# Finishing a mixture-of-experts block: last weights in two transfers, residual carried into the accumulators, final norm read from PSUM

## The reference, cut to what matters

```python
def moe_swiglu(h, router, w1, w3, w2):
    ...
    gate = jnp.sum(jax.nn.one_hot(top_i, N_EXPERTS, dtype=jnp.float32) * top_p[..., None], axis=1).astype(h.dtype)
    y = jnp.zeros_like(t)
    for e in range(N_EXPERTS):
        y = y + gate[:, e:e + 1] * swiglu(t, w1[e], w3[e], w2[e])
    return y.reshape(b, s, d)
...
            x = x + moe_swiglu(h, moe_router[j], moe_w1[j], moe_w3[j], moe_w2[j])
    return rmsnorm(x, final_norm_g)
```

## Time and profile before

| | us |
|---|---|
| median of 3 runs | 1676.49 |
| lowest and highest | 1676.17, 1682.53 |
| profiled execution, first to last instruction (span) | 1673.1 |
| end of the last scaling by VectorE in it | 1670.04 |

### The profile page before, as it was taken

One profiled execution on the slowest core, in us unless ns is written; L12 is line 12 of the kernel. 1 busy time (PEld: TensorE's weight loads), 2 busy tenths in 40 slices (PEclk: granted clock), 3 DMA queues, 4 the chain that ended last, 5 costly groups with the idle time before them and its releaser, 6 DMA issues.

```text
span 1673.1 us, 34751 instructions
## 1 busy us (share of the span) xinstructions
PE 1614.6 (97%) x15676; PEld 1089.6 (65%) x15676; DVE 612.5 (37%) x1036; ACT 446.8 (27%) x693; POOL 32.3 (2%) x27
## 2 busy tenths in 40 slices
PE   6999999999999999999999999999999999899995
PEld 6987776899988987776866534565345643356431
DVE  3678775554644677766501010101101010010101
ACT  3564533453534554523201010000100010000101
POOL 0000030000000000030000000000000000000000
PEclk9999999999999999999999999999999999999998
DMA  6424312454654433413989999999999999999994
GB/s 254 177 101 149 140 60 106 153 201 165 243 197 142 162 124 132 146 52 134 429 307 353 383 429 428 424 427 425 428 427 425 424 427 427 427 426 424 426 429 168
DMA packets 41108, 472.75 MB, mean 283 GB/s; under 512 B 4544, under 2 KB 4544, under 8 KB 5632
## 3 DMA queue, kind: packets, MB, share of 16 engines
q1 hardware_dynamic: 40592, 468.86, 69.6%
q0 software_dynamic: 368, 1.65, 0.2%
HBM read 469.44 MB, written 1.05 MB: 281 GB/s over the span
## 4 chain that ended last, share of the span: by engine, by line
PE 85%; DMA 7%; DVE 4%; ACT 2%; issue 1%; SPq 0%; DVEq 0%; ACTq 0%
PE bank L608 72%; DMA pairs_high<-stream 4%; DMA pairs_low<-stream 2%; PE bank L1221 1%; PE bank L1285 1%; PE bank L690 1%; DVE ring_a_r L1708 1%; DVE arena L1708 1%; PE bank L984 1%; ACT high_a L1378 1%; DMA smalls<-small 1%; PE bank L895 1%; PE bank L976 1%; PE bank L804 0%; PE bank L1246 0%
## 5 line engine op out<-in xcount | busy, mean ns | idle before, releaser
L608 PE MATMUL bank<-pairs_high,hsel 128*32 128x256 f32 (+1 forms) x4320 | 334.6, 408 | 2.8 <-DMA pairs_high<-stream 2.8
L608 PEld LDWEIGHTS bank<-pairs_high,hsel 128*32 128x32 f32 (+1 forms) x4320 | 161.7, 113 | 159.9 <-issue 83.2
L1708 DVE TENSOR_TENSOR ring_a_r<-ring_a,high_a 128x2048 fp32r<-128x2048 f32 x82 | 188.0, 2297 | 125.7 <-ACT high_a L1378 125.6
L1708 DVE TENSOR_TENSOR arena<-arena,bank 128x256 f32<-128x256 f32 (+2 forms) x122 | 44.5, 392 | 464.2 <-ACT arena L1631 451.4
L1378 ACT ACTIVATE high_a<-ring_a 128x2048 fp32r<-128x2048 f32 x82 | 157.1, 1916 | 134.4 <-PE bank L608 117.1
L608 PE MATMUL bank<-pairs_high,actT 128*32 128x256 f32 (+1 forms) x2048 | 165.2, 413 | 7.7 <-DMA pairs_high<-stream 7.7
L608 PE MATMUL bank<-hT_h,ring_a_r 128*128 128x256 f32 (+1 forms) x592 | 167.4, 283 | 0.0
L608 PE MATMUL bank<-high_a,hT_h 128*128 128x512 f32 (+1 forms) x416 | 165.1, 397 | 0.8 <-issue 0.8
L608 PE MATMUL bank<-pairs_low,hsel 128*32 128x256 f32 (+1 forms) x1952 | 161.9, 415 | 0.2 <-DMA pairs_low<-stream 0.2
L608 PE MATMUL bank<-high_a,hT_l 128*128 128x512 f32 (+1 forms) x416 | 160.1, 385 | 0.0
L608 PE MATMUL bank<-ring_a_r,hT_h 128*128 128x512 f32 (+1 forms) x416 | 160.1, 385 | 0.0
(11 more groups left out here) (324 smaller groups left out, 1784.5 us busy)
## 6 DMA issues: line engine op xcount, KB each, us to landing
pairs_high<-stream SPq DMA_DIRECT2D x113, 2048.0 KB, 27.2
pairs_low<-stream SPq DMA_DIRECT2D x55, 2048.0 KB, 27.2
ring_a<-stream SPq DMA_DIRECT2D x107, 1024.0 KB, 4.8
consts<-const SPq DMA_DIRECT2D x1, 1079.0 KB, 7.1
resid<-x SPq DMA_DIRECT2D x1, 1024.0 KB, 4.9
y<-xn SPq DMA_DIRECT2D x2, 512.0 KB, 2.6
smalls<-small SPq DMA_DIRECT2D x1, 824.5 KB, 10.6
smalls<-small POOLq DMA_DIRECT2D x1, 824.5 KB, 7.0
```

What stands on the lines that cost most here:

```text
L608: ins = mm(o, lhsT, rhs, start=start, stop=stop)
L1708: return v.tensor_tensor(o, i0, i1, op)
```

## The change

It has four parts.

1. The last pair of weights of place 7 comes in two transfers of 1 MB: the first piece with a semaphore of its own (`last_half_in`), the second with the pair's. `down` waits for each piece by itself there.
2. For narrow places ScalarE rounds straight from `pb[4]` and VectorE subtracts straight from `pb[4]`. VectorE's copy to `yexp` goes.
3. Before place 7's `down`, `carry` brings the residual into banks 0 to 3: four fp32 matmuls of the identity by `x`, 128 x 512 each, with start and no stop. `scatter_last` adds the twelve scatter products of both tiles to these four banks with no wait between the tiles. The adds to `x` go.
4. ScalarE squares each half from PSUM, four squares in place of two, and VectorE prepares the bias of the root from the first half's sum (`final_half`). VectorE scales from PSUM, two instructions a tile in place of one. A root of the constant one stands on ScalarE behind place 7's last `turned`, ahead of the evacuation, and again at the end of the overflow branch. The overflow branch also copies the banks back to `x` and carries `x` in again at its end.

```diff
+            if n == PIECES - 2:
+
+                sp.dma_start(pair(n)[:, 0:PIECE], src[:, 0:PIECE]).then_inc(sem("last_half_in"), 16)
+                sp.dma_start(pair(n)[:, PIECE:2 * PIECE], src[:, PIECE:2 * PIECE]).then_inc(piece_in(n), 16)
+            else:
+                sp.dma_start(pair(n), src).then_inc(piece_in(n), 16)
...
+                if n == PIECES - 2 and e is None:
+                    pe.wait_ge(sem("last_half_in"), 16)
+                elif n == PIECES - 1 and e is None:
+                    arrived(n, e)
+                elif c % 2 == 0:
+                    arrived(n, e)
...
+        def carry(start_only):
+            for tt in range(TT):
+                for half in range(2):
+                    ins = mm(pb[2 * tt + half][:, :], ident, x[:, tt, half * 512:half * 512 + 512], start=True, stop=not start_only)
+            return ins
+
+        def scatter_last(tt):
+            for lhs, rhs in ((pickT_h, yexp_h[0]), (pickT_h, yexp_l), (pickT_l, yexp_h[0])):
+                for half in range(2):
+                    hs = slice(64 * half, 64 * half + 64)
+                    ins = mm(pb[2 * tt + half][:, :], lhs[hs, tsl(tt)], rhs[hs, 0:512], start=False, stop=lhs is pickT_l)
+                    if lhs is pickT_l:
+                        ins.then_inc(sem("main_scattered"), 1)
...
+            if e is None and k == EXPERTS - 1:
+                carry(True)
             down(tag, first, wide, k, e)
...
-            act_e.wait_ge(sem(tag + "yexp"), s + 1)
...
+            else:
+                act_e.wait_ge(sem(tag + "down"), s + 1)
+                ins = a(yexp_h[0], pb[4][:, :], ACT.Copy)
...
+        root = stat[:, 140:141]
+        a(root, c_("one"), ACT.Sqrt)
         yexp_high("main_", EXPERTS - 1, WIDE[-1], sum(WIDE[:-1]))
...
-            act_e.wait_ge(sem("x_fed"), TT + tt + 1)
-            link(a(hT_flat[tt], x[:, tt, :], ACT.Square, accum_out=stat[:, tt:tt + 1]))
-            a(stat[:, 2 + tt:3 + tt], stat[:, tt:tt + 1], ACT.Sqrt, bias=c_("eps"), scale=1.0 / D).then_inc(sem("norm_std"), 1)
+            for half in range(2):
+                act_e.wait_ge(sem("main_scattered"), 4 * (EXPERTS - 1) + 2 * tt + half + 1)
+                at = 136 + 2 * tt + half
+                a(hT_flat[tt][:, half * 512:half * 512 + 512], pb[2 * tt + half][:, :], ACT.Square, accum_out=stat[:, at:at + 1])\
+                    .then_inc(sem("final_square"), 1)
+            act_e.wait_ge(sem("final_square"), 2 * tt + 2)
+            act_e.wait_ge(sem("final_half"), tt + 1)
+            a(stat[:, 2 + tt:3 + tt], stat[:, 137 + 2 * tt:138 + 2 * tt], ACT.Sqrt, bias=stat[:, tt:tt + 1], scale=1.0 / D).then_inc(sem("norm_std"), 1)
...
-                ins = v.tensor_copy(yexp[:, 0:512], pb[4][:, :])
...
+                ins = tt_(yexp_l[:, 0:512], pb[4][:, :], yexp_h[0].bitcast(F32), ALU.subtract)
...
-        for tt in range(TT):
-            add("main_", EXPERTS - 1, tt)
...
         for tt in range(TT):
+            ve.wait_ge(sem("final_square"), 2 * tt + 1)
+            ts(stat[:, tt:tt + 1], stat[:, 136 + 2 * tt:137 + 2 * tt], 1.0 / D, ALU.mult, EPS, ALU.add).then_inc(sem("final_half"), 1)
             ve.wait_ge(sem("norm_std"), TT * 2 * LAYERS + tt + 1)
             link(v.reciprocal(stat[:, 4 + tt:5 + tt], stat[:, 2 + tt:3 + tt]))
-            stt(xn[:, tt, :], x[:, tt, :], stat[:, 4 + tt:5 + tt], final_g, ALU.mult, ALU.mult).then_inc(sem("out_ready"), 1)
+            for half in range(2):
+                cols = slice(half * 512, half * 512 + 512)
+                ins = stt(xn[:, tt, cols], pb[2 * tt + half][:, :], stat[:, 4 + tt:5 + tt], final_g[:, cols], ALU.mult, ALU.mult)
+            ins.then_inc(sem("out_ready"), 1)
```

More of the change, by code:

```diff
@@ L558, in load_pair @@
             src = stream[n:n + 2] if p is None else stream[bass.ds(p * EXP_PIECES + (FIRST_EXPERT + j), 2)]
-            sp.dma_start(pair(n), src.rearrange("a p n -> (a p n)").rearrange("(p n) -> p n", p=P)).then_inc(piece_in(n), 16)
+            src = src.rearrange("a p n -> (a p n)").rearrange("(p n) -> p n", p=P)
+            if n == PIECES - 2:
[3 more added lines that the diff above has]
+                sp.dma_start(pair(n), src).then_inc(piece_in(n), 16)
         sp.wait_ge(sem("merged"), 2 * LAYERS)
@@ L1291, in down @@
                 n = first + 4 * EXP_GROUPS + c
+                if n == PIECES - 2 and e is None:
[4 more added lines that the diff above has]
+                    arrived(n, e)
                 if c % 2 == 0:
-                    arrived(n, e)
                     pe.wait_ge(sem(tag + "actT"), k * EXP_GROUPS + (c // 2 + 1))
@@ L1339, in _ @@
         yexp_ready("main_", EXPERTS - 1)
+        assert not WIDE[-1]
         for tt in range(TT):
-            scatter("main_", EXPERTS - 1, WIDE[-1], tt)
+            scatter_last(tt)
         pe.wait_ge(sem("over_known"), 1)
@@ L1359, in _ @@
                 scatter("over_", OVERS, True, tt)
+            pe.wait_ge(sem("over_added"), 4 * (OVERS + 1))
+            carry(False).then_inc(sem("over_carried"), 1)
     @block.scalar
@@ L1655, in yexp_high @@
                 act_e.wait_ge(sem(tag + "yexp_more"), o + 1)
-            act_e.wait_ge(sem(tag + "yexp"), s + 1)
-            rows = slice(0, HOLD if wide else P)
-            for half in range(2 if wide else 1):
-                ins = a(yexp_h[half][rows, :], yexp[rows, half * 512:half * 512 + 512], ACT.Copy)
+                act_e.wait_ge(sem(tag + "yexp"), o + 1)
+                for half in range(2):
+                    ins = a(yexp_h[half][0:HOLD, :], yexp[0:HOLD, half * 512:half * 512 + 512], ACT.Copy)
+            else:
+                act_e.wait_ge(sem(tag + "down"), s + 1)
+                ins = a(yexp_h[0], pb[4][:, :], ACT.Copy)
             ins.then_inc(sem(tag + "yexp_hi"), 1)
@@ L1689, in _ @@
             yexp_high("over_", OVERS, True, OVERS)
+            a(root, c_("one"), ACT.Sqrt)
+            act_e.wait_ge(sem("over_carried"), 1)
         for tt in range(TT):
-            act_e.wait_ge(sem("x_fed"), TT + tt + 1)
-            link(a(hT_flat[tt], x[:, tt, :], ACT.Square, accum_out=stat[:, tt:tt + 1]))
-            a(stat[:, 2 + tt:3 + tt], stat[:, tt:tt + 1], ACT.Sqrt, bias=c_("eps"), scale=1.0 / D).then_inc(sem("norm_std"), 1)
+            for half in range(2):
[6 more added lines that the diff above has]
+            a(stat[:, 2 + tt:3 + tt], stat[:, 137 + 2 * tt:138 + 2 * tt], ACT.Sqrt, bias=stat[:, tt:tt + 1], scale=1.0 / D).then_inc(sem("norm_std"), 1)
     @block.vector
@@ L2254, in yexp_in @@
         def yexp_in(tag, s, wide):
-            ve.wait_ge(sem(tag + "down"), s + 1)
             if wide:
+                ve.wait_ge(sem(tag + "down"), s + 1)
                 for r in range(THIRDS):
@@ L2261, in yexp_in @@
                                             pb[4 + r // 2][32 * q:32 * q + 32, 256 * (r % 2):256 * (r % 2) + 256])
-            else:
-                ins = v.tensor_copy(yexp[:, 0:512], pb[4][:, :])
[L2264 to L2269, removed]
+                ins.then_inc(sem(tag + "yexp"), 1)
+            ve.wait_ge(sem(tag + "yexp_hi"), s + 1)
+            if wide:
+                for half in range(2):
+                    cols = slice(half * 512, half * 512 + 512)
+                    ins = tt_(yexp_l[0:HOLD, cols], yexp[0:HOLD, cols], yexp_h[half][0:HOLD, :].bitcast(F32), ALU.subtract)
+            else:
+                ins = tt_(yexp_l[:, 0:512], pb[4][:, :], yexp_h[0].bitcast(F32), ALU.subtract)
             ins.then_inc(sem(tag + "yexp_lo"), 1)
@@ L2314, in _ @@
         yexp_in("main_", EXPERTS - 1, WIDE[-1])
-        for tt in range(TT):
-            add("main_", EXPERTS - 1, tt)
         more = ve.value_load(over_i[0:1, 0:1], min_val=0, max_val=1)
         with ve.If(more > 0):
-            ve.wait_ge(sem("main_added"), 4 * EXPERTS)
+            ve.wait_ge(sem("main_added"), 4 * (EXPERTS - 1))
+            for tt in range(TT):
+                for half in range(2):
+                    ve.wait_ge(sem("main_scattered"), 4 * (EXPERTS - 1) + 2 * tt + half + 1)
+                    ins = v.tensor_copy(x[:, tt, half * 512:half * 512 + 512], pb[2 * tt + half][:, :])
+            ins.then_inc(sem("over_x"), 1)
+            ve.wait_ge(sem("over_x"), 1)
             def choose_over(at):
@@ L2331, in _ @@
                 add("over_", OVERS, tt)
-        ve.wait_ge(sem("main_added"), 4 * EXPERTS)
-        for tt in range(TT):
-            v.tensor_copy(stat[:, 136 + tt:137 + tt], c_("one")).then_inc(sem("x_fed"), 1)
+            ve.wait_ge(sem("over_carried"), 1)
         ve.wait_ge(sem("final_in"), 16)
         for tt in range(TT):
+            ve.wait_ge(sem("final_square"), 2 * tt + 1)
+            ts(stat[:, tt:tt + 1], stat[:, 136 + 2 * tt:137 + 2 * tt], 1.0 / D, ALU.mult, EPS, ALU.add).then_inc(sem("final_half"), 1)
             ve.wait_ge(sem("norm_std"), TT * 2 * LAYERS + tt + 1)
             link(v.reciprocal(stat[:, 4 + tt:5 + tt], stat[:, 2 + tt:3 + tt]))
```

(5 more changed lines are left out.)

## The result

Over 20 runs each, the changed kernel has a median of 1671.64 us and the one before 1678.84 us: 7.20 us less. The ratio is 0.9963 with a 95% interval of 0.9950 to 0.9977, that is a gain of 6.2 us, between 3.9 and 8.4 (the ratio is an estimate of its own and not the quotient of the two medians). It is small and clear of zero. The prediction's 7.12 us is inside; its 1669.4 us lies 2.2 us under the median of 1671.64, because it started from the first three runs of the kernel before (1676.49), which over 20 runs is 2.35 us slower.

What follows compares the result with a forecast made beforehand. The stream of weights was taken to bound the kernel, leaving only its tail: gains of 1.43, 0.75, 4.75 and 1.28 us less 0.24 and 0.85 make 7.12, so 1676.49 becomes 1669.4 us, range 1667.6 to 1672.2.

Steps and rivals of the forecast that it cites:

- the yardstick: Whole kernel time: half a per cent, 8.4 us, is about what measurement can tell from no change; chance within it 0.83.
- A distance that was not kept: From the last scaling to the end of the span, the store: 3.06 us, taken as unchanged.
- Part 1: End of place 7's `down`: splitting the last weight pair lets PE work through without a wait, gaining 1.43 us.
- Rival B: Last weight pair: the second half pays its completion time again, 1.2 us is lost, 1670.6 us; chance 0.09.
- Part 3, the carry: Ahead of place 7's `down`: four matmuls take 3.57 us, made up by the fourth pair, so they cost zero.
- the limit of 6.8 us: Waits ahead of the pairs in place 7's `down`: they hide the residual's matmuls only up to about 6.8 us.
- Part 2: Between the end of `down` and the scatter: dropping the copy and rounding from the bank gains 0.75 us.
- Scatter and norm: Behind `down`: PE's scatter start to first square 1.00 us, was 5.75; 0.24 and 0.85 us given back in squares and later.
- The table load: ScalarE before the norm's root: the load moves into idle time, gaining 1.28 us; the skill's rule would give 2.66 us.
- rival C: ScalarE before the norm: the table load is put in again behind the overflow branch, 1.28 us, 1670.7 us; chance 0.12.
- Rival D: Tail: small terms together gain 1.3 us more than summed, time under 1668.1 us; chance 0.14.
- Rival E: Place 7's `down`: PE's clock falls to 0.50, about 1694 us; chance 0.03, with all else that makes it slower.

Runs made afterwards that it cites:

- the second profile of the changed kernel: The changed kernel run and profiled again with nothing edited; 1670.97 us over 12 runs, ratio 0.9966 against the kernel before.
- the third: The changed kernel profiled once more with nothing edited; ratio 0.9972 over 10 runs against the kernel before.
- The run with part 1 alone: The kernel before with only the last weight pair split into two transfers, each piece waited for by itself; ratio 1.0001.
- the one with part 2 alone: The kernel before with only the narrow places rounded and subtracted straight from PSUM, without the copy; 1673.84 us, one run.
- the one without the early roots: The changed kernel without the two early roots of the constant one; 1669.74 us over 12 runs, ratio 0.9962 against the kernel before.
- the first profile: The first profiled execution of the changed kernel, nothing further edited; span 1669.1 us.
- the run on eight shares: The changed kernel with the last weight pair in 16 transfers of 8 neighbouring partitions each; ratio 1.0042 against the kernel before.
- the run with the bias moved: The changed kernel with the second tile's bias put on VectorE between the first tile's two scalings; 1677.75 us, one run.
- the two on eight shares: The changed kernel with the last pair in 16 transfers of 8 partitions, neighbouring (ratio 1.0042) or 16 apart (1695.49 us, one run).

## Why the prediction was right or wrong

**The step that failed is the yardstick.** "Half a per cent is 8.4 us, about what a measurement of this kernel can tell from no change" put 0.83 on a change within it. That figure was worked out from no row. The median difference, 7.20 us, is 0.43% and lies within it, but 20 runs on each side give a ratio of 0.9950 to 0.9977, an interval 0.27 points wide, and no change is outside it. A forecast of 7.12 us was a forecast of a gain, small but real, and its text should have said so. The median, 1671.64, lies in the stated range of 1667.6 to 1672.2. That 7.20 comes within 0.1 us of 7.12 is luck: the interval is 4.5 us wide, and two things that the sum left out take away from the gain, as follows.

**A distance that was not kept.** The prediction took the 3.06 us from the last scaling to the end of the span, the store, as unchanged. In the three profiles of the changed kernel it is 4.3, 3.6 and 4.1 us. The pages' rows of the store, before and after (KB, and median us from issue to landing), show it:

```profile
y<-xn SPq DMA_DIRECT2D x2, 512.0 KB, 2.6
```

```profile
y<-xn SPq DMA_DIRECT2D x2, 512.0 KB, 4.2
```

So of the 7.42 us that the tail lost between the kernel before and the second profile (17.36 to 9.94) the span lost 6.90, and 6.58 by the third. The run with part 1 alone and the one with part 2 alone have 2.7 and 2.6 us as before, and so nearly has the one without the early roots, 2.8. In the packet records a fetch of 16 KB on the instruction queue begins within 1.4 us of the store's first packet, mostly within 0.3, wherever the store is slow (3.6 to 4.2 us), and 1.3 us or more ahead of it in the four others. That this is the cause was not tested.

**Part 1** was sized right at 1.43 us: 1.44 from the sixth pair's landing to the end of `down`, 1.50 by the tails of the split alone and of the change without it. The reason was right as well: PE's own pace takes over, and the end of `down` is the sixth pair's landing plus 7.15 us. What the step left out, and the second thing that takes from the gain, is that a landing at the very end can be late. Where the stall of the stream falls there, the end of `down` moves with it, and a longer idle time can take PE's clock with it (1.3 and 1.7 us in the first profile; 2.90 us of idle time in the run on eight shares did not). The fixed cost of each DMA by the Trainium skill (DMA: Bandwidth & Descriptors, section "Anatomy of one DMA") is about 2.0 us, and that section gives it for DMAs issued by GpSimd, while SyncE issues these. It does not speak against the split: the second half landed 2.46 to 2.47 us behind the first in all eight profiles with this split, which is 1 MB at the stream's pace to 0.04 us. Rival B is out.

**Part 3, the carry**, cost nothing: 3.60 us (forecast 3.57), level by the fourth pair. Doubled to 7.03 us it used up the waits ahead of the sixth pair, as the limit of 6.8 us said. **Part 2** was 0.76 us (0.75), by the run with it alone.

**Scatter and norm.** By the second profile of the changed kernel: scatter to the first square 1.01 us (1.00), which makes the largest term of the sum 4.74 (4.75); it is read from the two chains, and no run has the carried residual and the joined scatter alone. Twelve scatter products in 1.67 us where 1.9 to 2.7 were given, since the clock stayed up where it had fallen before. The fall goes with the wait between the two tiles. In the run with part 2 alone, with 1.42 us of idle time in front and 1.37 between, the second scatter was at the low clock as before; in all ten profiles with 1.42 in front and none between, the twelve products took 1.66 or 1.67 us. Then two squares 1.27 us (1.42: the second starts before the first one's sum is read out), two scalings 1.41 us (1.36), the wait for the bias 0.52 us (0.5). In sum 7.73 us from the end of `down` against 7.97. **The table load** was 1.28 us and gone for good; rival C fell with the first chain after.

**Rival D** (over 0.5% faster) did not come, though two of its small terms did (squares overlapping 0.15; the bias, once taken away, 0.5). **Rival E** (clock in `down`) showed up once in the three profiles of the changed kernel: one fall, 1.7 us, not the 15.5 it needed.

## What to carry to other kernels

When a stream bounds a kernel, count the time from its last landing to the end: that tail is the only part the compute engines own, and each step of it can be priced from the chain before touching it; here the forecast of the tail was off by 0.3 us in 10. Then go on to the end of the span: the store behind it, taken as unchanged, cost up to 1.3 us more. Splitting the last transfer gains little more than the idle time in front of it (1.4 us for 1.2 idle), since the consumer's own pace is next. Work of 3.6 us that fits into waits ahead of the end is free, but count the limit. And compare a forecast with the interval that the planned number of runs will give, not with a rule of thumb.

## What the runs showed of the hardware

- The stream of 2 MB transfers lands every 4.9 us, with 7 to 23 irregular spacings of 5.1 to 6.5 us from 1000 us on, in every kernel; the cause is open.
- The 16 shares of one transfer land up to 14 us apart while the stream is at its full 427 GB/s, eight of them (by the last pair of the kernel before) 10 to 12 us ahead of the other eight, and it ends with some 11 us at half rate. Handing the last pair to eight shares cost 14 and 18 us.
- PE's clock stayed at full with 1.2 us of idle time in every 4.9, with 1.45 and 1.90 us once, and with 2.90 and 2.52 us in the run on eight shares; behind 2.53 us in the changed kernel's first profile it fell to 1.2 GHz for 3.4 us.
- Most of the spread of the spans comes from PE's clock ahead of the experts. A window of the kernel before, and below it the same window of the run with the bias moved, whose span is 1676.0 us (PE's granted clock is the third figure from the end):

```profile
832.00:852.00 20.00, 20.00 (x303) 13.99 (x305) 3.74 (x17) 0.55 (x2) 0.00 (x0) 1.00 0.62 230
```

```profile
832.00:852.00 20.00, 20.00 (x155) 16.31 (x157) 6.55 (x31) 0.00 (x0) 0.00 (x0) 0.78 0.47 200
```

The granted clock falls at the same places of the program, near 113, 612 and 825 us and in some executions near 530 too, but for longer in one than in another: by the clock's records 17 us at 1.2 GHz ahead of the experts in the kernel before, 37.5 in the other, whose last weights landed 9.7 us later. The other profiles line up with these, the two on eight shares left aside: with 17 us (six of them) the last weights land at 1652.0 to 1653.6, with 20, 24, 31 and 34 us at 1653.6, 1656.8, 1657.9 and 1659.8. That is more than the whole change is worth.
